# The order of steps in differential attention's slots: scaling first, turns ahead of logits in every fourth slot, memory evictions one slot sooner, the last key turn later

## The chip, the cores and the metric

The kernel runs on one core of a Trainium2 chip. The metric is device time in microseconds (us) of one execution; lower is better. TensorE (PE in the profile) multiplies and turns (transposes) tiles, ScalarE (ACT) computes exponentials and copies, VectorE (DVE) does two-operand arithmetic and reductions, GpSimd (POOL) small extra work, and SyncE (SP) issues most of the transfers. Each engine runs its own list of instructions in order, and semaphores tie the lists together.

## What is computed

Two transformer blocks in a row on 512 tokens of width 1024, in float32. The first has two layers; the change lies in its second layer, which has differential attention (6 heads, two logit maps each) beside attention to a memory of 256 rows (4 heads). Cut to what matters:

```python
def diff_attention(q1, q2, k1, k2, v, lam):          # per block of 128 queries
        s1 = jnp.einsum('bqhd,bkhd->bhqk', a1, k1).astype(jnp.float32) * scale
        s2 = jnp.einsum('bqhd,bkhd->bhqk', a2, k2).astype(jnp.float32) * scale
        p1 = jax.nn.softmax(jnp.where(mask, s1, -jnp.inf), axis=-1)
        p2 = jax.nn.softmax(jnp.where(mask, s2, -jnp.inf), axis=-1)
        p = (p1 - lam * p2).astype(v.dtype)
        return jnp.einsum('bhqk,bkhe->bqhe', p, v)

def memory_attention(q, mem_n, w_mem_kv, q_gain, k_gain):
    sc = jnp.einsum('bshd,bmhd->bhsm', qh, k).astype(jnp.float32) * (MEM_HEAD_DIM ** -0.5)
    p = jax.nn.softmax(sc, axis=-1).astype(v.dtype)
    o = jnp.einsum('bhsm,bmhd->bshd', p, v)
```

## The kernel before

Large products are float32 in effect: each operand is split into a high and a low part, and a product is three matmuls (`mm3`, lines 1092 to 1094). ScalarE makes the high parts of the weights (line 1759), VectorE the low parts (lines 2252 and 2254).

The second layer's attention runs as a list of slots, `PLAN_B`. In each slot TensorE first does one piece of a projection (query, key, value, or output product; `PIECES`, at most four in a row share a weight slab), and then the steps that the list gives for that slot. ScalarE and VectorE walk the same list, each doing its own share of the same steps in the same order. They also take a share of the weights' splitting in every second slot.

The steps of the list:

- Memory attention, units 0 to 7: `s` logits, `x` exponential, `y` scaling, `t` turn of the weights (TensorE line 1216, ScalarE line 1820, VectorE line 2317), `v` product with the values, `e` eviction of it (ScalarE line 1832, VectorE line 2324). A pair of units shares one `v` and one `e`.
- `rt` turns rotated rows of queries or keys, one 128-row tile at a time, on TensorE (line 1436), and ScalarE takes the result (line 2000).
- Differential attention, units 0 to 23; unit u is query tile u % 4 of head u // 4, and works on 128, 256, 384 or 512 keys. `D`: two logit products on TensorE (lines 1455 and 1458), then the maxima on VectorE (lines 2637 and 2641). `X`: the two exponentials on ScalarE (line 2026), then on VectorE the reciprocals of the sums (lines 2646 and 2649). `M`: ScalarE scales the second map (line 2015), then VectorE combines both (line 2654). `T`: TensorE turns the combined weights (line 1464), ScalarE makes the high part (line 2008), VectorE the low part (line 2659). `V`: product with the values, after which `O` (ScalarE lines 2032 and 2035) takes it out.
- Once a head: `sums` (TensorE line 1418), `R` (a reciprocal root over ScalarE lines 1771 and 1773 and VectorE), `N` (TensorE line 1486, VectorE line 2673), `C` (ScalarE line 2043), and the residual's `add` (VectorE line 2684).

`unit_at(s)` gives unit s its slot. Units 0 to 7 come three slots apart. Units 8 to 23 are dense: four units in six slots. In each such group of four, the logits stand in the first, second, fourth and fifth slot, and the exponential in the slot after its logits, ahead of the next unit's logits where both meet. `D` of a unit waits for `X` of the unit before, since both use the same two PSUM banks (`q.wait_ge(S("df_exp"), 2 * u)`, line 1445). `T`, `t`, `rt` and `N` share one PSUM bank in the list's order: each of them waits until the one before it has been read out. ScalarE's `O` waits for TensorE's `V`, and VectorE's `M` for ScalarE's `M`.

Of the kernel before, what the change touches and what calls it, by code (L numbers as in the profile page):

```python
# [15 lines left out]
T = 512  # L16
D = 1024
# [80 lines left out]
def build(nc, cols, ins, out):  # L98
# [10 lines left out]
    def place(shape, dt, offset):  # L109
        names[0] += 1  # L110
        return nc.alloc_sbuf_tensor_at(f"sb{names[0]}", shape, dt, offset=offset)
# [303 lines left out]
    PLAN_B = [[] for _ in range(len(PIECES) + 8)]  # L415
    KEY_ROWS = 69

    def unit_at(s):
        return 44 + 3 * s if s < 8 else 74 + (s - 8) * 3 // 2 if s < 24 else 97 + (s - 24) * 3 // 2
# [8 lines left out]
    for t in range(4):  # L428
        PLAN_B[16 + t].append(("qt", t))
        PLAN_B[24 + 3 * t].append(("rt", "QB", t))  # L430
        PLAN_B[(38, 39, 41, 42)[t]].append(("rt", "KB", t))
        PLAN_B[52 + t].append(("rt", "QA", t))
        PLAN_B[71 + t + (t > 0)].append(("rt", "KA", t))
        PLAN_B[77 + t].append(("ev", "va", t))
    for u in range(8):
        s = 20 + 3 * u
        PLAN_B[s].append(("s", u))
        PLAN_B[s + 1].append(("x", u))
        PLAN_B[s + 2].append(("y", u))
        PLAN_B[s + 5].append(("t", u))  # L440
        if u % 2 == 1:
            PLAN_B[s + 7].append(("v", u // 2))
            PLAN_B[s + 8].append(("e", u // 2))
    for s in range(30):
        p = unit_at(s)
        if s >= 4 and s % 4 == 0 and s <= 24:
            PLAN_B[p].append(("V", s // 4 - 1, 0))
        if s >= 8 and s % 4 == 0:
            PLAN_B[p].append(("sums", s // 4 - 2))
        if s < 24:  # L450
            PLAN_B[p].append(("D", s))
        if 0 <= s - 2 < 24:
            PLAN_B[p].append(("T", s - 2))
        if 0 <= s - 1 < 24:
            PLAN_B[p].append(("M", s - 1))
        if s < 24:
            PLAN_B[p + 1].append(("X", s))
        if s >= 6 and s % 4 == 2:
            PLAN_B[p + 1].append(("V", s // 4 - 1, 1))
        if s >= 6 and s % 4 == 2:  # L460
            PLAN_B[p + 1].append(("O", s // 4 - 1))
        if s >= 8 and s % 4 == 0:
            PLAN_B[p + 1].append(("R", s // 4 - 2))
        if s >= 9 and s % 4 == 1:
            PLAN_B[p + 1].append(("N", s // 4 - 2))
            PLAN_B[p + 2].append(("C", s // 4 - 2))
# [354 lines left out]
    KA = place([128, 4, 512], F32, s1_off)  # L821
# [2171 lines left out]
```

## Time and profile before

| | us |
|---|---|
| median of 3 runs | 1722.68 (1721.58 to 1723.02) |
| the profiled execution | 1722.6 |
| its span, first to last instruction | 1720.8 |
| TensorE busy | 1680.7 |
| VectorE busy | 1222.5 |
| ScalarE busy | 842.6 |
| the stretch of the second layer's attention | about 540 to 780 us in the span |

The profile is of one execution. Busy time of an engine is the time in which it has an instruction under way; TensorE's clock is given beside it as a share of full speed (mean 0.994). In the rows, a start is counted from the span's start; a number in brackets behind a row is how long the engine had been idle, with what ended the wait.

### The profile page before, as it was taken

What the parts mean: (1) busy time and instruction counts of PE and PEld (TensorE: products, weight loads), DVE (VectorE), ACT (ScalarE), POOL (GpSimd) and SP (SyncE); (2) the same over time, 40 slices, a digit from 0 to 9 for tenths busy, and PEclk for the clock granted to TensorE, in tenths of its full rate; (3) what the DMA queues carried; (4) which work ended last, traced back from release to release, by engine and by line L of the source; (5) the groups of instructions that cost most, each with busy time, mean ns of one, the idle gap of its engine ahead of it and who ended that gap; (6) DMA issues with size and microseconds to landing.
All of it is one profiled execution on the core that took longest, in us unless ns stands there. A gap on an engine that the chain in (4) does not pass through costs nothing.

```text
span 1720.8 us, 20867 instructions
## 1 busy us (share of the span) xinstructions
PE 1680.7 (98%) x7882; PEld 1373.8 (80%) x7882; DVE 1222.5 (71%) x1868; ACT 842.6 (49%) x1405; POOL 62.8 (4%) x116
## 2 busy tenths in 40 slices
PE   7999999999999999899999999999999999999998
PEld 6778888888888777668888888888877788888886
DVE  6667458687888666765777778988885645766666
ACT  7444344343445776764444444555876523333342
POOL 0000000000001121000000000013100000000000
PEclk9999999999999999999999999999989999999999
DMA  9322443333412212116142424058500262234212
GB/s 329 86 74 93 140 123 95 111 92 107 132 52 51 77 51 73 40 47 187 47 146 62 149 69 124 13 128 192 115 26 25 87 209 73 63 122 123 71 46 79
DMA packets 200500, 169.02 MB, mean 98 GB/s; under 512 B 5776, under 2 KB 161808, under 8 KB 200144
## 3 DMA queue, kind: packets, MB, share of 16 engines
q1 hardware_dynamic: 194816, 157.31, 29.8%
q0 software_dynamic: 4576, 8.85, 2.9%
q10 hardware_dynamic: 1008, 1.53, 0.3%
q8 instruction: 63, 1.03, 0.2%
q14 instruction: 37, 0.30, 0.1%
HBM read 157.96 MB, written 2.10 MB: 93 GB/s over the span
## 4 chain that ended last, share of the span: by engine, by line
PE 90%; DVE 5%; ACT 3%; issue 1%; DMA 0%; POOL 0%; DVEq 0%; SPq 0%; ACTq 0%
PE ps L1092 28%; PE ps L1094 28%; PE ps L1093 28%; PE ps L1156 1%; PE ps L1455 1%; PE ps L1575 1%; DVE sb L2254 1%; ACT sb L1759 1%; PE ps L1587 1%; ACT sb L2026 1%; DVE sb L2733 1%; PE ps L1109 0%; DVE sb L2782 0%; PE ps L1110 0%; PE ps L1113 0%
## 5 line engine op out<-in xcount | busy, mean ns | idle before, releaser
L1092 PE MATMUL ps<-sb,sb 128*128 128x512 f32 (+2 forms) x2292 | 887.9, 390 | 11.6 <-DVE sb L2254 10.1
L1094 PE MATMUL ps<-sb,sb 128*128 128x512 f32 (+2 forms) x2292 | 874.5, 383 | 0.0
L1093 PE MATMUL ps<-sb,sb 128*128 128x512 f32 (+2 forms) x2292 | 873.9, 383 | 0.0
L2254 DVE TENSOR_TENSOR sb<-sb,sb 128x1024 fp32r<-128x1024 f32 (+1 forms) x414 | 405.1, 998 | 223.5 <-ACT sb L1759 223.0
L1759 ACT ACTIVATE sb<-sb 128x1024 fp32r<-128x1024 f32 (+1 forms) x414 | 349.1, 870 | 386.1 <-PE ps L1094 380.1
L1092 PEld LDWEIGHTS ps<-sb,sb 128*128 128x128 f32 (+1 forms) x2292 | 429.4, 189 | 105.2 <-DVE sb L2254 10.8
L1094 PEld LDWEIGHTS ps<-sb,sb 128*128 128x128 f32 (+1 forms) x2292 | 429.0, 188 | 84.8
L1093 PEld LDWEIGHTS ps<-sb,sb 128*128 128x128 f32 (+1 forms) x2292 | 429.5, 189 | 80.7
L2485 DVE TENSOR_TENSOR sb<-sb,sb 128x1024 fp32r<-128x1024 f32 x70 | 85.5, 1222 | 47.5 <-ACT sb L1933 45.2
L1928 ACT ACTIVATE sb<-sb 128x512 f32<-128x512 f32 x64 | 40.3, 631 | 131.3 <-DVE sb L2537 131.3
L2467 DVE TENSOR_TENSOR sb<-sb,sb 128x1024 f32<-128x1024 f32 x80 | 95.2, 1218 | 0.6
L2502 DVE TENSOR_TENSOR sb<-ps,sb 128x512 f32<-128x512 f32 x120 | 76.1, 682 | 0.3 <-PE ps L1094 0.3
L2733 DVE SCALAR_TENSOR_TENSOR sb<-sb,sb,sb 128x512 f32<-128x512 f32 x90 | 67.4, 749 | 2.0
L1933 ACT ACTIVATE sb<-sb 128x1024 fp32r<-128x1024 f32 x56 | 58.7, 1048 | 9.0 <-DVE sb L2479 8.9
L2537 DVE SCALAR_TENSOR_TENSOR sb<-ps,sb 128x512 f32<-128x512 f32 x64 | 43.6, 685 | 9.0 <-PE ps L1094 9.0
L2479 DVE TENSOR_TENSOR sb<-sb 128x1024 f32<-128x1024 f32 x40 | 48.7, 1218 | 0.1
L2210 ACT ACTIVATE sb<-sb 128x512 f32<-128x512 f32 x22 | 13.9, 632 | 70.6 <-DVE sb L2912 70.5
L1069 POOL DMA_DIRECT2D sb<-sb x29 | 25.1, 879 | 430.9 <-ACT sb L2101 390.1
L2252 DVE SCALAR_TENSOR_TENSOR sb<-sb,sb,sb 128x512 fp32r<-128x512 f32 x40 | 29.6, 751 | 11.8 <-ACT sb L1759 11.6
L1765 ACT ACTIVATE sb<-sb 128x1024 f32<-128x1024 f32 x26 | 27.5, 1059 | 8.5 <-DVE sb L2684 4.9
L2026 ACT ACTIVATE sb<-ps,sb,sb 128x128 f32<-128x128 f32 (+3 forms) x48 | 29.1, 613 | 5.1 <-DVE sb L2641 5.1
L2912 DVE TENSOR_TENSOR sb<-ps,sb 128x512 f32<-128x512 f32 x22 | 15.1, 687 | 20.8 <-PE ps L1094 20.8
(215 smaller groups left out, 1167.7 us busy)
## 6 DMA issues: line engine op xcount, KB each, us to landing
sb<-in_w_up SPq DMA_DIRECT2D x86, 512.0 KB, 4.0
sb<-in_w_down SPq DMA_DIRECT2D x86, 512.0 KB, 4.8
sb<-in_w_gate SPq DMA_DIRECT2D x22, 512.0 KB, 3.9
sb<-in_a_w_in SPq DMA_DIRECT2D x20, 512.0 KB, 3.8
sb<-in_w_in SPq DMA_DIRECT2D x20, 512.0 KB, 3.8
sb<-in_w_o SPq DMA_DIRECT2D x16, 512.0 KB, 3.7
sb<-sb POOLq DMA_DIRECT2D x29, 256.0 KB, 4.6
sb<-in_w_mem_kv SPq DMA_DIRECT2D x8, 512.0 KB, 8.7
```

The source lines that it names most:

```text
L1092: mm(ps, lh, rh, start=start, stop=False, **k)
L1093: mm(ps, lh, rl, start=False, stop=False, **k)
L1094: return mm(ps, ll, rh, start=False, stop=stop, **k)
L1759: act(WH[i % N_SPLIT][:, a], raw[:, a], ACT.Copy, scale=g).then_inc(S("w_hi"), parts)
L1933: act(AR[(7 * g + j) % 4][0], a_of(l, g, j)[0], ACT.Copy).then_inc(S("h_hi"), 1)
L2026: act(E, banks[B.lb + w][:, 0:nk], ACT.Exp, bias=M[:, 2 + w:3 + w], scale=r[:, w:w + 1], accum_out=M[:, 4 + w:5 + w]).then_inc(S("df_exp"), 1)
L2254: tt(lo, raw, hi, ALU.subtract).then_inc(S("w_lo"), parts)
L2467: tt(db[d][a][:, :], db[b][a][:, :], db[c][a][:, :], ALU.subtract).then_inc(S("t_sum"), 1)
L2479: tt(d, x, y, op).then_inc(S("hs"), 1)
L2485: tt(lo, a_of(l, g, j)[0], hi.bitcast(F32), ALU.subtract).then_inc(S("h_lo"), 1)
L2502: tt(x, y, x, ALU.add).then_inc(S("res"), 1)
L2733: stt(CV[:, j, :], GL[:, j, k:k + T], col("convw", 4 * k + j), CV[:, j, :], ALU.mult, ALU.add).then_inc(S("tap"), 1)
```

## The change

The change alters only the list `PLAN_B`; every instruction stays, with the same operands.

```diff
-        PLAN_B[71 + t + (t > 0)].append(("rt", "KA", t))
+        if t < 3:
+            PLAN_B[71 + t + (t > 0)].append(("rt", "KA", t))
...
         if u % 2 == 1:
-            PLAN_B[s + 7].append(("v", u // 2))
-            PLAN_B[s + 8].append(("e", u // 2))
+            PLAN_B[s + 7] += [("v", u // 2), ("e", u // 2)]
     for s in range(30):
         p = unit_at(s)
+        if 0 <= s - 1 < 24:
+            PLAN_B[p].append(("M", s - 1))
         if s >= 4 and s % 4 == 0 and s <= 24:
             PLAN_B[p].append(("V", s // 4 - 1, 0))
         if s >= 8 and s % 4 == 0:
             PLAN_B[p].append(("sums", s // 4 - 2))
-        if s < 24:
-            PLAN_B[p].append(("D", s))
-        if 0 <= s - 2 < 24:
-            PLAN_B[p].append(("T", s - 2))
-        if 0 <= s - 1 < 24:
-            PLAN_B[p].append(("M", s - 1))
+        unit = [("D", s)] if s < 24 else []
+        turned_ = [("T", s - 2)] if 0 <= s - 2 < 24 else []
+        PLAN_B[p] += turned_ + unit if s % 4 == 1 else unit + turned_
         if s < 24:
             PLAN_B[p + 1].append(("X", s))
+        if s == 8:
+            PLAN_B[p + 1].append(("rt", "KA", 3))
```

So `M` of the unit before goes from the end of a slot's unit steps to their start; `T` goes ahead of `D` for units 1, 5, 9 and so on; the memory evictions `e` go one slot sooner, into the slot of their product `v`; and the last turn of keys goes behind `X` of unit 8 within its slot. The changed file has one line more, so its line numbers are one higher from there on.

TensorE, around the logits of unit 17, before (line 1455 and 1458 are `D`, 1464 is `T`; the 1092 row starts the next piece):

```order
3147 L1093 MATMUL ps<-sb_62,sb_167 128x512
3148 L1094 MATMUL ps<-sb_59,sb_168 128x512
3149 L1455 MATMUL ps<-sb_153,sb_151 128x256 x2
3150 L1458 MATMUL ps<-sb_70,sb_69 128x128 x2
3151 L1464 MATMUL ps<-sb_64,sb_127 128x128 x4
3152 L1092 MATMUL ps<-sb_60,sb_125 128x512
```

And in the changed kernel:

```order
3147 L1094 MATMUL ps<-sb_62,sb_167 128x512
3148 L1095 MATMUL ps<-sb_59,sb_168 128x512
3149 L1465 MATMUL ps<-sb_64,sb_127 128x128 x4
3150 L1456 MATMUL ps<-sb_153,sb_151 128x256 x2
3151 L1459 MATMUL ps<-sb_70,sb_69 128x128 x2
3152 L1093 MATMUL ps<-sb_60,sb_125 128x512
```

The turn of unit 15 now stands ahead of the logits of unit 17.

VectorE, from the reciprocals of unit 17 to those of unit 19, before (2637 and 2641 are the maxima of `D`, 2659 is `T`, 2654 is `M`, 2673 is `N`):

```order
756 L2649 TENSOR_SCALAR sb_147<-sb_147,sb_144 128x1
757 L2673 SCALAR_TENSOR_TENSOR sb_135<-ps,sb_144,sb_133 128x512
760 L2637 TENSOR_REDUCE sb_147<-ps 128x1 x2
762 L2659 TENSOR_TENSOR sb_130<-ps,sb_129 128x128
763 L2654 SCALAR_TENSOR_TENSOR sb_127<-sb_127,sb_147,sb_128 128x256
...
765 L2649 TENSOR_SCALAR sb_147<-sb_147,sb_144 128x1
766 L2637 TENSOR_REDUCE sb_147<-ps 128x1 x2
767 L2641 SCALAR_TENSOR_TENSOR sb_147<-sb_147,sb_146 128x2
768 L2659 TENSOR_TENSOR sb_130<-ps,sb_129 128x2x128
769 L2654 SCALAR_TENSOR_TENSOR sb_127<-sb_127,sb_147,sb_128 128x384
```

And in the changed kernel:

```order
756 L2650 TENSOR_SCALAR sb_147<-sb_147,sb_144 128x1
757 L2674 SCALAR_TENSOR_TENSOR sb_135<-ps,sb_144,sb_133 128x512
760 L2655 SCALAR_TENSOR_TENSOR sb_127<-sb_127,sb_147,sb_128 128x256
761 L2638 TENSOR_REDUCE sb_147<-ps 128x1 x2
763 L2660 TENSOR_TENSOR sb_130<-ps,sb_129 128x128
...
765 L2650 TENSOR_SCALAR sb_147<-sb_147,sb_144 128x1
766 L2655 SCALAR_TENSOR_TENSOR sb_127<-sb_127,sb_147,sb_128 128x384
767 L2638 TENSOR_REDUCE sb_147<-ps 128x1 x2
768 L2642 SCALAR_TENSOR_TENSOR sb_147<-sb_147,sb_146 128x2
769 L2660 TENSOR_TENSOR sb_130<-ps,sb_129 128x2x128
```

The combination of units 17 and 18 now stands ahead of the maxima of units 18 and 19.

ScalarE, around the second memory eviction, before (1842 is `x`, 1832 is `e`, 1820 is `t`, 1827 is `y`):

```order
376 L1773 ACTIVATE sb_77<-sb_77 128x4
377 L1842 ACTIVATE sb_148,sb_147<-ps,sb_147,sb_145 128x256 x2
378 L1759 ACTIVATE sb_58<-sb_57,sb_65 128x512
379 L1832 ACTIVATE sb_125<-ps 64x256 x2
380 L1820 ACTIVATE sb_149<-ps 128x4x128
381 L1827 ACTIVATE sb_148<-sb_148,sb_147 128x256 x2
```

And in the changed kernel:

```order
376 L1774 ACTIVATE sb_77<-sb_77 128x4
377 L1833 ACTIVATE sb_125<-ps 64x256 x2
378 L1843 ACTIVATE sb_148,sb_147<-ps,sb_147,sb_145 128x256 x2
379 L1760 ACTIVATE sb_58<-sb_57,sb_65 128x512
380 L1821 ACTIVATE sb_149<-ps 128x4x128
381 L1828 ACTIVATE sb_148<-sb_148,sb_147 128x256 x2
```

The eviction now stands ahead of the exponential of memory unit 5; the same holds for the other three.

## Rows read from the trace of the kernel before

**Rows 1.** The page, section 1: busy time, share of the span, instructions.

```profile
PE 1680.7 (98%) x7882; PEld 1373.8 (80%) x7882; DVE 1222.5 (71%) x1868; ACT 842.6 (49%) x1405; POOL 62.8 (4%) x116
```

**Rows 2.** Waits of TensorE, 540 to 790 us: total, times, longest (us).

```profile
PE ps L1455 <- ACT sb L2026: 3.7, 4, 1.7
PE ps L1486 <- DVE sb L2659: 2.4, 4, 0.8
PE ps L1436 <- DVE sb L2317: 1.9, 1, 1.9
```

**Rows 3.** Stretches, TensorE: length, busy (count), granted clock, DMA share, GB/s.

```profile
613.00:617.00 4.00, 4.00 (x14) 0.57 0.22 72
690.00:692.00 2.00, 0.38 (x4) 1.00 0.00 0
```

**Rows 4.** Timeline of the group of units 16 to 19: start, length, instruction.

```profile
724.24 0.95 PE L1418 MATMUL ps<-sb,sb 128*128 128x2 f32 x8
...
728.22 0.70 PE L1455 MATMUL ps<-sb,sb 64*128 64x256 f32 x4 [0.68 <-ACT sb L2026]
...
730.09 0.39 ACT L2015 ACTIVATE sb<-sb,sb 128x128 f32<-128x128 f32 x1
...
730.11 0.76 DVE L2637 TENSOR_REDUCE sb<-ps 128x1 f32<-128x256 f32 x2
...
730.97 0.69 DVE L2659 TENSOR_TENSOR sb<-ps,sb 128x512 fp32r<-128x512 f32 x1
...
731.72 0.65 PE L1486 MATMUL ps<-sb,sb 128*128 128x128 f32 x4 [0.75 <-DVE sb L2659]
...
733.60 0.63 ACT L2043 ACTIVATE sb<-sb 128x512 fp32r<-128x512 f32 x1 [0.78 <-DVE sb L2673]
...
734.71 1.02 DVE L2637 TENSOR_REDUCE sb<-ps 128x1 f32<-128x384 f32 x2
...
737.69 1.13 PE L1455 MATMUL ps<-sb,sb 64*128 64x512 f32 x4
...
738.42 0.63 ACT L2035 ACTIVATE sb<-sb 128x512 f32<-128x512 f32 x1
...
738.91 1.29 DVE L2637 TENSOR_REDUCE sb<-ps 128x1 f32<-128x512 f32 x2 [1.09 <-PE ps L1458]
...
739.56 0.61 ACT L2015 ACTIVATE sb<-sb,sb 128x384 f32<-128x384 f32 x1
...
740.59 0.77 ACT L2026 ACTIVATE sb<-ps,sb,sb 128x512 f32<-128x512 f32 x1
...
742.60 0.95 PE L1418 MATMUL ps<-sb,sb 128*128 128x2 f32 x8
```

**Rows 5.** Timeline: the sums that open units 12 to 15, and those behind unit 23.

```profile
705.62 1.05 PE L1418 MATMUL ps<-sb,sb 128*128 128x2 f32 x8
...
760.80 1.05 PE L1418 MATMUL ps<-sb,sb 128*128 128x2 f32 x8 [0.49 <-ACT sb L2026]
...
764.31 0.63 PE L1464 MATMUL ps<-sb,sb 128*128 128x128 f32 x4 [0.68 <-DVE sb L2654]
```

**Rows 6.** Timeline around the first two memory products.

```profile
593.52 0.56 ACT L1842 ACTIVATE sb<-ps,sb,sb 128x256 f32<-128x256 f32 x1
...
594.25 0.28 PE L1094 MATMUL ps<-sb,sb 128*128 128x256 f32 x1
...
600.64 0.46 ACT L2000 ACTIVATE sb<-ps,sb 128x256 f32<-128x256 f32 x1
...
612.06 0.44 PE L1436 MATMUL ps<-sb,sb 128*128 128x128 f32 x2 [1.93 <-DVE sb L2317]
```

**Rows 7.** Timeline around units 1 to 3 and the query turns.

```profile
634.77 0.55 ACT L2026 ACTIVATE sb<-ps,sb,sb 128x256 f32<-128x256 f32 x1
...
642.92 0.66 PE L1436 MATMUL ps<-sb,sb 128*128 128x128 f32 x4 [0.23 <-DVE sb L2659]
...
648.77 0.66 PE L1436 MATMUL ps<-sb,sb 128*128 128x128 f32 x4 [0.16 <-DVE sb L2659]
```

## What was predicted

> **What bounds the kernel now.** The page comes first: TensorE is busy for 98% of the span, VectorE 71% [rows 1]. So an edit is worth what it does to TensorE's idle time and clock. The change adds and removes no instruction, so only waits can move. The waits of TensorE over the second layer's attention come next. Three kinds matter [rows 2]: logits `D` that wait for the exponential of the unit before (3.7 us, 4 times), the turn `N` that waits for VectorE's half of `T` (2.4 us, 4 times), and one query or key turn `rt` that waits 1.9 us for VectorE's half of a memory turn `t`. Then the clock by stretches: behind the 1.9 us wait it is 0.57 over 4 us, which costs 4 x 0.43 = 1.7 us on top, while a wait of 1.66 us inside 690 to 692 left it at 1.00 [rows 3]. The timeline of one dense group, last, shows what stands around each wait [rows 4]. Some 12 us in all could be had.
>
> **The dense groups (units 8 to 23).** I take the group of units 16 to 19. It runs from its `sums` at 724.24 to the next at 742.60, 18.36 us [rows 4]. I walk the new order through it with the old durations, putting the start of `sums` at 0 and handing over between engines in 0.05 us (the `N` at 731.72 starts 0.06 after the end of the VectorE row at 730.97 [rows 4]). Next starts on one engine overlap the last by about 0.1 us.
>
> What it gains. `T` of unit 15 goes ahead of `D` of unit 17 and fills the wait of 0.68 us. `M` of unit 15 no longer holds up ScalarE ahead of `X` of unit 16. The next piece starts some 0.7 us sooner, and `N` follows about 0.6 us sooner, since the turn it waits for is earlier.
>
> What it costs. `D` on VectorE feeds the exponential and so the next `D` on TensorE; in the new order it stands behind `M`, and `M` on VectorE stands behind `M` on ScalarE.
>
> - Unit 17's maxima. Before, they start at 730.11, that is 5.87. Now ahead of them come, from the end of unit 16's reciprocals (about 5.2; VectorE has the split of a weight half and `R` there as before): ScalarE's `M` 0.39, its half of `T` (about 0.6), and VectorE's half of `T`, 0.69, which waits for it [rows 4]. 5.2 + 0.3 + 0.6 + 0.7 gives 6.8: 0.9 us later, and `X` of unit 17 with them.
> - Unit 18's maxima. Before 734.71, 10.47. `X` of unit 17 is late by 0.9, so its reciprocals, `N`'s VectorE part and ScalarE's `C` (0.63, before at 733.60 [rows 4]) are late: `C` starts about 10.2. `M` of unit 17 waits in line behind `C` on ScalarE, and VectorE's maxima wait for it. 10.2 + 0.5 (`C` less the overlap) + 0.5 + 0.5 (an estimate, between the 0.39 and 0.61 of units 16 and 18) gives 11.65: 1.2 us later. `X` of unit 18 then ends at 14.3, and `D` of unit 19 on TensorE starts at 14.35, against 13.45 before (737.69 [rows 4]). Here the gain of 0.7 is gone and 0.9 lost.
> - Unit 19's maxima. In this slot ScalarE also has `O`, two copies of 0.6 each (the second at 738.42 [rows 4]), and it stands ahead of `M`. Before, VectorE took unit 19's maxima at 738.91, straight from TensorE, while ScalarE was still at `O` and got to `M` at 739.56. Now: `X` of unit 18 ends 14.3, `O` to 15.45, `M` on ScalarE 0.61, `M` on VectorE as long, maxima at 16.55. Before it was 14.67. `X` of unit 19 starts 1.5 later (1.29 of maxima, the small product, a handover), at 18.07 against 16.35 before (740.59 [rows 4]), and lasts 1.6; the next `sums` waits for its end and starts at 19.73 against 18.36.
>
> So the group takes 1.4 us more. As a check from below: even if `X` of unit 18 came in time and TensorE kept its 0.7, `O` would end at 738.5 and `M` on both engines put unit 19's maxima at 739.65 instead of 738.91, 0.7 later; less 0.4 us that lie between the end of `X` and `sums` (740.59 + 1.6 = 742.2 against 742.60 [rows 4]) that still is about +0.25 us a group. A gain of a whole group isn't in reach.
>
> For the other groups: units 12 to 15 take 18.62 now (705.62 to 724.24) and get the same 19.73, +1.1; units 20 to 23 take 18.20 (742.60 to 760.80), +1.5 [rows 4, 5]. In units 8 to 11 ScalarE's evictions of values and the last key turn set the pace; the key turn behind `X` of unit 8 turns the 1.7 us wait [rows 2] into one of about 0.75, which brings TensorE forward by 1.1 us, and unit 11's late `M` takes it back: +0.1. Behind unit 23, `T` waits 0.68 us for `M` [rows 5], which is now ahead of the other steps: -0.7. Sum of the dense part: 0.1 + 1.1 + 1.4 + 1.5 - 0.7 = +3.4 us.
>
> **The memory evictions.** `e` on ScalarE now waits for the product `v` of its own slot, with `x` behind it. At the first, ScalarE was free at 593.52 and took `x`; `v` ends at 594.53 [rows 6]. ScalarE stalls 1.0 us in a stretch in which it is busy without a gap, so the taking out of a query turn at 600.64 [rows 6] comes 1.0 later, and TensorE's next user of that bank, the turn of memory unit 3 just behind it, waits 0.9. At the second, `e` fits into an idle time and leaves the slot where the 1.93 us wait ends at 612.06 [rows 6]: there ScalarE saves 0.7 and VectorE 0.9. With the 0.9 from before, TensorE gets through at about 611.8: -0.3, and the wait shrinks to 0.8. As 1.66 us left the clock at full speed [rows 3], I take the 1.7 us of half clock as gone: -1.7. At the fourth, `e` waits 1.3 us for `v` and takes 0.7, and `X` of unit 1, at 634.77 before [rows 7], starts 2.0 later. VectorE and ScalarE are full for the next 6 us there. The maxima of unit 2 come 1.5 us later (0.4 of it for `M` of unit 1 ahead), unit 0's turn behind them, and the query turn at 642.92, which already waits for that turn, with it: +1.45. `M` of unit 2 ahead of unit 3's maxima adds another 0.65 at the turn at 648.77 [rows 7]. Together -0.3 - 1.7 + 2.1 = +0.1.
>
> Bounds. Where a stall of ScalarE is absorbed, the query turns cost nothing, not +2.1; where nothing is, the first eviction's 0.9 adds to it. The half clock returns 0 or 1.7, or a new stretch costs another 1.7. The dense part lies between four times the 0.25 from below, less 0.7, and four times 1.5: +0.3 to +6.
>
> **The clock.** The row at 690 to 692 says that a wait of 1.66 us can pass at full clock, and the new waits in a dense group are at most 1.1 [rows 3]. The Trainium skill ("TensorE: Matmul & The Clock Gate", Part 1: The HAM clock gate) says that the throttled state is the default and activity releases it; by that alone each group with more idle time than before could lose its clock once. With one half-clock stretch a group of 1.7 us the sum would be 3.5 + 4 x 1.7, some 1733; by the row it is nothing. I go by the row.
>
> **The sum.** +3.4 + 0.1 = +3.5 us on the profiled 1722.6, 1726.1; on the median of 1722.68, which is 0.1 above it, 1726.2. A difference of 0.2%, 3.4 us, is about what a measurement of this kernel tells from no change, and the forecast lies on that edge.
>
> **The rivals.**
>
> - Half the delay is absorbed (chance 0.27). VectorE is at 71%, and other steps may close up behind `M` sooner than I walk. Then the dense groups cost about 0.7 each and the query turns 1: 4 x 0.7 - 0.7 + 1 - 2 = +1.1, 1723.8. For it: no step is longer, only the order. Against: each link of the walk is a wait that the list makes.
> - A clock loss (0.17). The half-clock stretch stays where it is, or comes back beside the query turn at 642.9, whose wait grows to about 1.7 us, the length of the wait that just passed. 1726.2 + 1.7 = 1727.9. It decides as soon as a wait is as long as the 1.93 of now.
> - The turns ahead fill their waits and nothing is lost (0.08). It needs `M` to be ready before the maxima in each slot, that is ScalarE at least 1.2 us sooner in the slot with `O`. Then the four waits of `D` (3.7), half of those of `N` (1.2), the 0.7 behind unit 23, and the 2.0 at the memory turn are all gained: -7.6, 1715.
> - The forecast itself, delays of 1 to 1.5 us in three groups with the half clock gone: 0.48.
>
> **How the numbers follow.** The forecast and the clock rival span 1724.5 to 1729.3; the absorbed case reaches down to 1722.3. 1722.3 to 1729.3 leaves out the gain of the third rival and the tails of the others, about 2 in 10. Faster by over 0.2% only by the third rival and none of the others: 0.08. Slower: the clock rival nearly whole, 0.15, and a little over half of the forecast, 0.28: 0.43. Within 0.2%: the rest, 0.49.
>
> **What would show it right or wrong.** Right: from one `sums` to the next 19.7 us instead of 18.4 and 18.2 in the groups of units 16 and 20; the maxima of the 512-key units released by ScalarE's `M` and no longer by TensorE; `D` of the 512-key unit waiting about 1 us for ScalarE; clock at 1.00 from 613 to 617. Wrong: periods at or under 18.4 (the absorbed case or the gain), a key or query turn without waits at 642.9 and 648.8, or a clock under 1.00 anywhere between 640 and 760.

## The result and the profile after

| kernel | median (us) | runs | profiled span (us) |
|---|---|---|---|
| before | 1722.85 (1721.58 to 1724.78) | 4 | 1720.8 |
| after | 1731.47 (1730.44 to 1732.40) | 4 | 1728.9 |

The change makes the kernel slower: ratio 1.0055, 95% interval 1.0043 to 1.0067. The prediction said 1726.2, with 1729.3 as the upper end of its range. It gave slower by more than 0.2% a chance of 0.43, faster 0.08, and no clear change 0.49. So the direction that it leaned to was right, though it was not its likeliest outcome. The size was off by 5.3 us, and the range missed.

The page of the kernel after has nearly the same busy times as [rows 1], spread over 8.1 us more. In this kernel all line numbers are one higher than before.

```profile
PE 1681.5 (97%) x7882; PEld 1373.7 (79%) x7882; DVE 1224.6 (71%) x1868; ACT 842.9 (49%) x1405; POOL 63.2 (4%) x116
```

The waits of TensorE from 540 to 790 us, against [rows 2]: total, times, longest.

```profile
PE ps L1456 <- ACT sb L2027: 4.4, 4, 2.0
PE ps L1437 <- DVE sb L2660: 2.5, 2, 1.7
PE ps L1487 <- DVE sb L2660: 2.3, 3, 0.8
PE ps L1093 <- POOL sb L1064: 2.0, 2, 1.0
PE ps L1419 <- ACT sb L2027: 1.2, 4, 0.4
PE ps L1437 <- DVE sb L2318: 1.1, 1, 1.1
PE ps L1093 <- DVE sb L2660: 1.1, 1, 1.1
```

`D` waits longer (L1456), `sums` waits at the end of every group (L1419), the query turns wait (L1437 on L2660), and a kind that was not there before appears: a piece of a weight product (L1093) waits for GpSimd (L1064, the low part of a head's output). It is 2.0 us, and the prediction has no word about it.

The stretches of TensorE, against [rows 3]: length, busy time, granted clock, DMA share, GB/s.

```profile
613.00:617.00 4.00, 4.00 (x22) 1.00 0.38 121
762.00:766.00 4.00, 2.96 (x15) 1.00 0.00 0
766.00:768.00 2.00, 1.12 (x8) 1.00 0.00 0
768.00:772.00 4.00, 4.00 (x17) 0.57 0.02 4
```

The half clock at 613 to 617 is gone, as predicted. But one of the same length and depth, 0.57 over 4 us, now stands at 768 to 772, so that nothing is gained by it.

The timeline of the group of units 16 to 19, against [rows 4]: start, length, instruction.

```profile
731.96 0.40 ACT L2016 ACTIVATE sb<-sb,sb 128x128 f32<-128x128 f32 x1 [0.75 <-DVE sb L2650]
...
736.87 0.63 ACT L2044 ACTIVATE sb<-sb 128x512 fp32r<-128x512 f32 x1 [0.69 <-DVE sb L2674]
...
737.35 0.68 DVE L2255 TENSOR_TENSOR sb<-sb,sb 128x512 fp32r<-128x512 f32 x1
737.41 0.49 ACT L2016 ACTIVATE sb<-sb,sb 128x256 f32<-128x256 f32 x1
737.58 1.60 POOL L1064 TENSOR_TENSOR sb<-sb,sb 128x512 fp32r<-128x512 f32 x1 [19.12 <-ACT sb L2044]
...
737.95 1.51 DVE L2655 SCALAR_TENSOR_TENSOR sb<-sb,sb,sb 128x256 f32<-128x256 f32 x1
739.38 1.01 DVE L2638 TENSOR_REDUCE sb<-ps 128x1 f32<-128x384 f32 x2
...
742.09 1.13 PE L1456 MATMUL ps<-sb,sb 64*128 64x512 f32 x4 [2.04 <-ACT sb L2027]
...
743.73 0.62 DVE L2655 SCALAR_TENSOR_TENSOR sb<-sb,sb,sb 128x384 f32<-128x384 f32 x1 [1.24 <-ACT sb L2016]
...
744.26 1.28 DVE L2638 TENSOR_REDUCE sb<-ps 128x1 f32<-128x512 f32 x2
```

The row to see is the one at 737.95. VectorE's half of `M` of unit 17 lasts 1.51 us, for 256 columns, while the 384 columns of unit 18 at 743.73 take 0.62. Its share on ScalarE was done at 737.90, so it began with its inputs ready, while GpSimd's subtraction of 737.58 was running, and it ended at 739.46, 0.28 us behind that one's end at 739.18. The maxima of unit 18 stand behind it, then `X`, then `D` of unit 19 at 742.09, which has waited 2.04 us. In the kernel before, VectorE had the maxima beside the same subtraction, with one input, from PSUM, and `M` only after its end (two more rows of before):

```profile
734.30 1.61 POOL L1063 TENSOR_TENSOR sb<-sb,sb 128x512 fp32r<-128x512 f32 x1 [17.33 <-ACT sb L2043]
...
736.05 0.47 DVE L2654 SCALAR_TENSOR_TENSOR sb<-sb,sb,sb 128x256 f32<-128x256 f32 x1
```

The four such `M` of the dense part take 1.14, 1.19, 1.51 and 1.19 us after, and 0.47 or 0.48 before.

In the other groups, and where `sums` opens units 20 to 23 and closes unit 23:

```profile
718.51 0.50 PE L1093 MATMUL ps<-sb,sb 128*128 128x512 f32 x1 [0.98 <-POOL sb L1064]
...
726.74 1.05 PE L1419 MATMUL ps<-sb,sb 128*128 128x2 f32 x8 [0.29 <-ACT sb L2027]
...
766.52 0.38 PE L1093 MATMUL ps<-sb,sb 128*128 128x256 f32 x1 [1.11 <-DVE sb L2660]
...
767.85 1.36 PE L1419 MATMUL ps<-sb,sb 128*128 128x2 f32 x8 [0.35 <-ACT sb L2027]
```

The time from one `sums` to the next leaves out what came before the dense part. Single profiles of kernels whose program is the same up to 685 us reach that point up to 1.2 us apart (685.07 in one of the runs below, 686.22 before), while their groups agree to 0.02 us. The table has these times for before, after and all runs, each from one profiled execution (the tail is from the `sums` behind unit 23 to the last one).

| kernel | 8–11 | 12–15 | 16–19 | 20–23 | tail | sum |
|---|---|---|---|---|---|---|
| before | 19.40 | 18.62 | 18.36 | 18.20 | 13.03 | 87.61 |
| after | 20.06 | 20.43 | 20.72 | 20.39 | 13.76 | 95.36 |
| e1 scaling last | 19.34 | 19.22 | 18.59 | 18.79 | 13.00 | 88.94 |
| e2 scaling first alone | 20.55 | 19.62 | 19.90 | 19.59 | 12.14 | 91.80 |
| e3 evictions alone | 19.41 | 18.64 | 18.35 | 18.20 | 13.03 | 87.63 |
| e4 after, GpSimd one fill | 19.38 | 19.71 | 19.69 | 19.67 | 12.15 | 90.60 |
| e5 after, GpSimd two fills | 19.39 | 19.98 | 19.69 | 19.95 | 12.14 | 91.15 |
| e6 turns ahead alone | 19.64 | 19.21 | 18.58 | 18.77 | 12.98 | 89.18 |
| e7 scaling first at a group's start | 18.01 | 18.27 | 17.75 | 17.58 | 12.13 | 83.74 |
| e8 after, not beside GpSimd | 18.98 | 20.15 | 19.32 | 20.12 | 13.52 | 92.09 |
| e9 key turn alone | 18.56 | 18.63 | 18.35 | 18.20 | 13.01 | 86.75 |
| e10 first beside the output copies | 19.88 | 19.37 | 19.19 | 19.37 | 13.73 | 91.54 |
| e11 e7, second eviction alone | 18.03 | 18.28 | 17.74 | 17.60 | 12.13 | 83.78 |
| e12 first beside GpSimd | 20.18 | 19.17 | 19.50 | 18.73 | 13.01 | 90.59 |

Of the 8.1 us, 7.75 lie here.

The table does not hold all of a kernel's time, and the medians show it: e1, e2 and e6 are 2.8, 7.6 and 3.1 us above before by their medians, but 1.3, 4.2 and 1.6 by the table. Part of the difference is TensorE's clock far behind this layer. Between 1250 and 1320 us it was at half in every profile for some microseconds. Its lost share times the length comes to 5.1 or 5.2 us in most, 6.8 in e1, e5, e6 and e11, and 10.3 in e10. Executions of one kernel differ in this way too: the five of e4 took 1725.6 to 1729.1 us, the slower two at a mean clock of 0.993 and the others at 0.994 or 0.995. Whether the change moves these later stretches, no run here separates. So the steps are read from the groups, and the medians only say faster or slower.

### The profile page after: what moved, and what is told of

Same layout as the page of the kernel before. It is cut to its first block, busy times and chain, and to the rows that moved or that the text cites. A ratio compares the mean times of both kernels' runs of the same rounds, so it can differ in the third digit from the quotient of the medians.

```text
span 1728.9 us, 20867 instructions
## 1 busy us (share of the span) xinstructions
PE 1681.5 (97%) x7882; PEld 1373.7 (79%) x7882; DVE 1224.6 (71%) x1868; ACT 842.9 (49%) x1405; POOL 63.2 (4%) x116
## 4 chain that ended last, share of the span: by engine, by line
PE 88%; DVE 6%; ACT 5%; issue 1%; DMA 0%; POOL 0%; DVEq 0%; SPq 0%; ACTq 0%
PE ps L1093 28%; PE ps L1095 27%; PE ps L1094 27%; ACT sb L2027 1%; DVE sb L2638 1%; PE ps L1576 1%; PE ps L1157 1%; PE ps L1588 1%; DVE sb L2255 1%; ACT sb L1760 0%; PE ps L1110 0%; PE ps L1111 0%; PE ps L1114 0%; DMA sb<-in_w_mem_kv 0%; DVE sb L2783 0%
## 5 line engine op out<-in xcount | busy, mean ns | idle before, releaser
L1093 PE MATMUL ps<-sb,sb 128*128 128x512 f32 (+2 forms) x2292 | 887.6, 390 | 14.6 <-DVE sb L2255 10.3
L1093 PEld LDWEIGHTS ps<-sb,sb 128*128 128x128 f32 (+1 forms) x2292 | 428.9, 188 | 109.5 <-DVE sb L2255 10.9
```

Source lines behind the costliest of these rows:

```text
L1093: mm(ps, lh, rh, start=start, stop=False, **k)
```

## The experiments

Theory: `M` first costs by the order, as walked, and by one thing that the walk did not have, VectorE and GpSimd reading SBUF at once (the clash, from here on). The rivals were that `T` ahead or the evictions carry the loss, or that GpSimd is only a bystander. Each ratio is to the kernel before, timed on the same chip in the same rounds; its median was 1722.03 beside e1 to e4, 1721.78 beside e5 to e8, and 1722.35 beside e9 to e12. Line numbers shift by up to five between runs, as the edits add or take lines.

### The parts: e1, e2, e3

e1 is the changed kernel with `M` back behind `D` and `T`:

```diff
-        if 0 <= s - 1 < 24:
-            PLAN_B[p].append(("M", s - 1))
         if s >= 4 and s % 4 == 0 and s <= 24:
...
         PLAN_B[p] += turned_ + unit if s % 4 == 1 else unit + turned_
+        if 0 <= s - 1 < 24:
+            PLAN_B[p].append(("M", s - 1))
```

> The changed kernel with one part undone: M goes back behind D and T in its slot; T ahead of D in every fourth slot, the earlier evictions and the later key turn stay. Theory A (M ahead of the maxima is the whole loss): the three dense groups of units 12 to 23 fall from 20.4 to 20.7 us each back to 18.4 or less, VectorE's scaling of the 256-key unit is back at 0.48 us, and the kernel ends 2 to 4 us below the kernel before (1719 to 1721), since the 1.7 us of half clock and the 0.7 us wait before the turn stay gained. Rival B (the turn ahead of the logits is what hurts, because VectorE's half of the turn now stands ahead of the maxima): periods stay above 19 us and the kernel at or above 1726.

Measured: 1724.86, ratio 1.0016 (1.0008 to 1.0025). It lies between the two, so neither expectation holds: most of the loss leaves with `M` first, but what stays is still a loss and not a gain. Its rows, on TensorE:

```profile
690.34 0.66 PE L1465 MATMUL ps<-sb,sb 128*128 128x128 f32 x4 [1.33 <-ACT sb L2001]
...
716.58 0.50 PE L1093 MATMUL ps<-sb,sb 128*128 128x512 f32 x1 [0.98 <-POOL sb L1064]
...
727.80 0.63 PE L1465 MATMUL ps<-sb,sb 128*128 128x128 f32 x4 [0.68 <-DVE sb L2655]
```

`T` of unit 15, moved ahead of `D` of unit 17 (the row at 727.80), waits for `M` for the same 0.68 us that `D` waited for `X` in [rows 4], and the piece that needs GpSimd's low part comes too soon. In units 8 to 11, `T` now stands right behind the last key turn and waits 1.33 us for ScalarE to take that turn's result (the row at 690.34).

e2 is the kernel before with `M` first and nothing else:

```diff
     for s in range(30):
         p = unit_at(s)
+        if 0 <= s - 1 < 24:
+            PLAN_B[p].append(("M", s - 1))
...
             PLAN_B[p].append(("T", s - 2))
-        if 0 <= s - 1 < 24:
-            PLAN_B[p].append(("M", s - 1))
```

> The kernel before with only M moved to the start of each slot's steps. Theory A: it alone brings most of the loss, periods of 19.5 us or more for units 12 to 23, VectorE's scaling of the 256-key unit 1.1 to 1.5 us long beside GpSimd's subtraction, and 4 to 8 us over the kernel before (1727 to 1731), with the half-clock stretch still near 613 us. Rival B: within 2 us of the kernel before.

Measured: 1729.60, ratio 1.0044 (1.0031 to 1.0058), and +4.2 us in the table's sum. The profiled execution, at 1726.63, was the fastest of its four. Theory A, with the half-clock stretch near 613 us still there (0.74 from 612 to 616). `M` first carries most of the loss by itself, and the scaling of the 256-key units is as long as in the changed kernel (1.12, 1.21, 1.51 and 1.21 us).

e3 is the kernel before with the evictions sooner and nothing else:

```diff
-            PLAN_B[s + 7].append(("v", u // 2))
-            PLAN_B[s + 8].append(("e", u // 2))
+            PLAN_B[s + 7] += [("v", u // 2), ("e", u // 2)]
```

> The kernel before with only the memory evictions one slot sooner. By the prediction's steps: the turn at 612 waits about 1.1 us instead of 1.9, the half clock behind it (1.7 us) is gone, a wait of about 0.7 us comes in at 601, and the query turn at 642.9 waits about 1.1 us longer without M's share: -1 us in all (1721.5 to 1722.5), or 1.7 higher if the half clock only moves. Rival (evictions sooner cost more than they bring): over 1724.5.

Measured: 1722.11, ratio 1.0004 (0.9995 to 1.0013), no difference. The half clock is gone, and most of its time went where the prediction put it, into a later query turn and into the wait at 601. First a stretch behind the turn, then the query turn in the timeline:

```profile
612.00:616.00 4.00, 4.00 (x25) 1.00 0.16 37
```

```profile
641.91 0.66 PE L1435 MATMUL ps<-sb,sb 128*128 128x128 f32 x4 [1.31 <-DVE sb L2658]
```

### The clash with GpSimd: e4, e5, e8, e12

e4 is the changed kernel in which GpSimd, instead of subtracting, fills the low part with zeros; the output lacks that part.

```diff
-                    TTT(lo[:, :], OT[:, :], hi[:, :].bitcast(F32), ALU.subtract).then_inc(S("sub_lo"), 1)
+                    e.memset(lo[:, :].bitcast(F32), 0.0).then_inc(S("sub_lo"), 1)
```

> The changed kernel with GpSimd's subtraction for the low part of each head's result (128x512, two inputs from SBUF) replaced by a fill with zeros, so the low part is left out of the output product. Theory C (VectorE's scaling stands still while GpSimd reads SBUF): VectorE's scaling of the 256-key unit falls from 1.14 to 1.51 us to 0.48, the periods of units 12 to 23 from 20.4 to 20.7 us to the 19.7 of the prediction's walk, and the kernel loses 2 to 3.5 us (1728 to 1729.5). Rival D (the scaling is long for another reason, such as its place behind the weight's split): it stays over 1.1 us and the kernel within 0.7 us of 1731.

Measured: 1726.44, ratio 1.0031 (1.0019 to 1.0043), and a span 5.2 us under that of after. Theory C in its rows, with more time lost than its 2 to 3.5 us, since the half clock of the tail went too. The scaling is back at 0.48, although it still starts while GpSimd is at work:

```profile
735.50 0.53 POOL L1064 MEMSET sb<- 128x512 f32 x1 [19.15 <-ACT sb L2044]
...
735.90 0.48 DVE L2655 SCALAR_TENSOR_TENSOR sb<-sb,sb,sb 128x256 f32<-128x256 f32 x1
```

One fill is shorter than the subtraction too, so that the low part also comes sooner. e5 makes it late again with a second fill behind the first, still without reading anything (and still without the low part in the output):

```diff
-                    TTT(lo[:, :], OT[:, :], hi[:, :].bitcast(F32), ALU.subtract).then_inc(S("sub_lo"), 1)
+                    e.memset(lo[:, :].bitcast(F32), 0.0).then_inc(S("fill"), 1)
+                    q.wait_ge(S("fill"), g + 1)
+                    e.memset(lo[:, :].bitcast(F32), 0.0).then_inc(S("sub_lo"), 1)
```

> The changed kernel with GpSimd's subtraction (the low part of a head's output, 1.3 to 1.6 us, two SBUF inputs) replaced by two fills of 0.53 us each, the second waiting for the first: GpSimd is busy about as long and its low part is as late as in the changed kernel, but it reads nothing. The output lacks that low part. In the run with one fill, VectorE's scaling of a 256-key unit took 0.48 us instead of 1.14 to 1.51, but the low part was also sooner, so two causes went at once. Theory A (both read SBUF and stand in each other's way): the scaling takes 0.48 us here too, D of the 512-key units waits 2.8 us in all and not 4.4; the pieces behind T still wait about 0.8 us twice for the low part; 1727 to 1728. Rival B (it is the late low part that costs, and the long scaling hides behind it): as the changed kernel, 1730 or more. Rival C (GpSimd's being at work stops VectorE, whatever it reads): the scaling stays above 1 us.

Measured: 1728.47, ratio 1.0044 (1.0028 to 1.0059), 0.5 us above theory A's range. Theory A's three rows came: the scaling takes 0.48, pieces wait 0.80 us twice for the low part, and `D` waits less (1.8 us in all, where 2.8 was expected). In the rows the scaling runs beside both fills:

```profile
736.40 0.53 POOL L1064 MEMSET sb<- 128x512 f32 x1 [18.85 <-ACT sb L2046]
736.80 0.48 DVE L2657 SCALAR_TENSOR_TENSOR sb<-sb,sb,sb 128x256 f32<-128x256 f32 x1
736.99 0.52 POOL L1066 MEMSET sb<- 128x512 f32 x1
```

So the two causes come apart. From e4 to e5 the table's sum grows by 0.55 us: that is the late low part. From e5 to after it grows by 4.2: 1.7 of it is the half clock of the tail, and the other 2.5 is left for the clash. Up to 0.4 of that can still be the low part, since two fills end a little sooner than the subtraction and the two waits for it are 0.80 and not 0.98 us. Rival C is out by the rows. Rival B is out by them too: `D` waits 1.8 us and not 4.4, and each group is 0.4 to 1.0 us shorter than in after. The medians alone would not settle B, as the intervals of the two ratios overlap. The Trainium skill ("SBUF — State Buffer", Who interferes with whom) has the rule: "A DVE instruction with two SBUF inputs contends with a GpSimd instruction that reads SBUF", and one that only writes does not. The trace agrees on all its sides: 1.14 to 1.51 us beside the subtraction, 0.48 beside fills, and 1.02 us, as everywhere, for maxima from PSUM beside it [rows 4].

e8 is the changed kernel with `M` behind again in the one slot of four in which GpSimd subtracts:

```diff
-        if 0 <= s - 1 < 24:
+        if 0 <= s - 1 < 24 and s % 4 != 2:
             PLAN_B[p].append(("M", s - 1))
...
         PLAN_B[p] += turned_ + unit if s % 4 == 1 else unit + turned_
+        if 0 <= s - 1 < 24 and s % 4 == 2:
+            PLAN_B[p].append(("M", s - 1))
```

> The changed kernel with M behind D and T again in one slot of four, that in which GpSimd subtracts (M of the 256-key unit). Theory A (that slot carries most of the loss): the scaling takes 0.48 us, D of the 512-key unit comes 2 us sooner and waits under 0.3, groups of 18.7 to 19.3 us instead of 20.4 to 20.7, 1725 to 1727. Rival B (the slot with O carries it): groups stay at 20 or more, 1729 to 1731.

Measured: 1729.08, ratio 1.0044 (1.0030 to 1.0058). Theory A is right in two groups (18.98 and 19.32 us) and wrong in the other two (20.15 and 20.12). There the piece behind `T` waits 0.98 us for the low part, as in after, and what the scaling gives back goes into that wait. The expectation had no term for it; the total came out outside its range.

e12 goes the other way, the kernel before with `M` first in that slot alone:

```diff
+        if 0 <= s - 1 < 24 and (s % 4 == 2):
+            PLAN_B[p].append(("M", s - 1))
...
-        if 0 <= s - 1 < 24:
+        if 0 <= s - 1 < 24 and not (s % 4 == 2):
             PLAN_B[p].append(("M", s - 1))
```

> The kernel before with M first in one slot of four, that in which GpSimd subtracts (M of the 256-key unit ahead of the maxima of the 384-key unit). Theory A (this slot costs by the order and by the clash with GpSimd): the scaling takes 1.1 to 1.5 us instead of 0.48, the maxima behind it come some 1.5 us later, D of the 512-key unit waits about 1 us, groups 0.7 to 1.2 us longer, 1725 to 1727. Rival B (TensorE's pieces cover it when T and the other M stand where they stood): groups within 0.3, under 1723.5.

Measured: 1725.81, ratio 1.0018 (1.0009 to 1.0027), groups longer by 0.78, 0.55, 1.14 and 0.53 us. Theory A, though two groups stay under its 0.7; `D` waits 6.4 us in all, against 3.7 before.

```profile
736.04 1.60 POOL L1065 TENSOR_TENSOR sb<-sb,sb 128x512 fp32r<-128x512 f32 x1 [17.88 <-ACT sb L2045]
736.41 1.51 DVE L2656 SCALAR_TENSOR_TENSOR sb<-sb,sb,sb 128x256 f32<-128x256 f32 x1
737.85 1.01 DVE L2639 TENSOR_REDUCE sb<-ps 128x1 f32<-128x384 f32 x2
740.55 1.13 PE L1457 MATMUL ps<-sb,sb 64*128 64x512 f32 x4 [1.06 <-ACT sb L2028]
```

### The other slots and steps: e6, e9, e10

e6 is the kernel before with `T` ahead of `D` in every fourth slot:

```diff
-        if s < 24:
-            PLAN_B[p].append(("D", s))
-        if 0 <= s - 2 < 24:
-            PLAN_B[p].append(("T", s - 2))
+        unit = [("D", s)] if s < 24 else []
+        turned_ = [("T", s - 2)] if 0 <= s - 2 < 24 else []
+        PLAN_B[p] += turned_ + unit if s % 4 == 1 else unit + turned_
```

> The kernel before with T ahead of D in every fourth slot alone. Theory A (T ahead gives no time back by itself: the wait of D moves behind it, and C is released by the exponential of unit 17 and no more by N, so that the low part is 1 us late for a piece in every second group): from one sums to the next about 0.6 us more in two or three of four groups, as in the run with scaling last, +1.3 in all; 1723.5 to 1724.5. Rival B (T fills the wait of D, and what the run with scaling last lost came from the key turn): groups of 17.7 to 18.0, 1720 to 1721.

Measured: 1724.92, ratio 1.0017 (1.0008 to 1.0026), groups longer by 0.24, 0.59, 0.22 and 0.57 us. Theory A, a little above its 1724.5. The two larger ones are those with the wait for the low part:

```profile
716.92 0.50 PE L1091 MATMUL ps<-sb,sb 128*128 128x512 f32 x1 [0.98 <-POOL sb L1062]
```

e10 is built as e12, with `s % 4 == 3`, the slot in which ScalarE copies the output twice.

> The kernel before with M first in one slot of four, that in which ScalarE copies the output twice (M of the 384-key unit ahead of the maxima of the 512-key unit). Theory A (what the prediction put as the least that this slot can cost: maxima 0.7 us later, 0.4 of it absorbed ahead of sums): groups 0.25 to 0.4 us longer, +1 to +1.6 in all, 1723.3 to 1724. Rival B (it is absorbed): groups as before within 0.1, 1722 to 1722.7. Rival C (the output slot carries the larger part of the loss): 0.8 us and more a group, above 1725.

Measured: 1726.89, ratio 1.0031 (1.0019 to 1.0043), groups longer by 0.48, 0.75, 0.83 and 1.17 us. It is nearer to rival C, against what I expected: above 1725, with 0.8 us a group as the mean of the four. (The profiled execution, at 1730.02, was the slowest of its six. Its tail holds a half-clock stretch too, 1.7 us.)

```profile
738.53 0.60 ACT L2034 ACTIVATE sb<-ps 128x512 f32<-128x512 f32 x1 [0.41 <-PE ps L1096]
739.16 0.63 ACT L2037 ACTIVATE sb<-sb 128x512 f32<-128x512 f32 x1
739.70 0.60 ACT L2017 ACTIVATE sb<-sb,sb 128x384 f32<-128x384 f32 x1
...
740.87 1.28 DVE L2639 TENSOR_REDUCE sb<-ps 128x1 f32<-128x512 f32 x2
```

The maxima start 16.00 us into the group (its `sums` is at 724.87) against 14.67 before, 1.33 later, and 0.83 arrives at the next `sums`. The 0.25 to 0.4 of the expectation was the prediction's check from below, which counted on TensorE keeping 0.7 us from `T` ahead; here there is none.

e9 is the kernel before with the last key turn behind `X` of unit 8:

```diff
-        PLAN_B[71 + t + (t > 0)].append(("rt", "KA", t))
+        if t < 3:
+            PLAN_B[71 + t + (t > 0)].append(("rt", "KA", t))
...
             PLAN_B[p + 1].append(("X", s))
+        if s == 8:
+            PLAN_B[p + 1].append(("rt", "KA", 3))
```

> The kernel before with the last key turn behind X of unit 8 alone. Theory A (the key turn held up ScalarE ahead of an exponential, as the prediction has it): the 1.66 us wait ahead of D of unit 9 shrinks to about 0.75 and the group of units 8 to 11 takes 18.3 us instead of 19.4, 1721 to 1722. Rival B (the wait only moves from D to the turn T behind it, as the 1.33 us in the run with scaling last suggests): the group takes 19.2 or more, no difference, 1722 to 1723. The run with scaling first at the group's start had 18.01 there, so by A nearly all of that gain is the key turn's, by B it is M's.

Measured: 1721.36, ratio 0.9992 (0.9983 to 1.0002); its group takes 18.56 us instead of 19.40. Theory A in kind, 0.84 us of the 1.1; `D` of unit 9 waits 0.23 us instead of 1.66, and `T` behind it 0.34. A gain of that size is under what the times resolve, but not under what the groups show.

### A faster version: e7, e11

e7 is the kernel before with the evictions (as e3), the key turn (as e9), and `M` first only in the slot that opens a group:

```diff
+        if 0 <= s - 1 < 24 and (s % 4 == 0):
+            PLAN_B[p].append(("M", s - 1))
...
-        if 0 <= s - 1 < 24:
+        if 0 <= s - 1 < 24 and not (s % 4 == 0):
             PLAN_B[p].append(("M", s - 1))
```

> The kernel before with the memory evictions one slot sooner and the last key turn later, and with M first only in the slots that open a group (M of units 11, 15, 19 and of the last unit), where no output copies stand on ScalarE and no subtraction on GpSimd; T stays behind D. Theory A (M first is paid for only beside O and beside GpSimd): D of the second unit of a group comes 0.3 us sooner, 4 times; T behind the last unit no longer waits 0.7; the evictions give 1.0; sum -2.9, 1719 to 1720. Rival B (M first costs in every slot, since the maxima stand behind it): groups 0.5 us longer each, 1723 or more.

Measured: 1717.89, ratio 0.9977 (0.9968 to 0.9986): faster, and by 1.1 us more than theory A's 1719. `D` of the second unit waits 0.3 us once, and otherwise not at all. In the third group it starts 3.36 us behind `sums`, against 3.98 before (728.22 less 724.24 [rows 4]), 0.6 sooner and not 0.3:

```profile
722.00 0.95 PE L1422 MATMUL ps<-sb,sb 128*128 128x2 f32 x8
...
725.36 0.70 PE L1459 MATMUL ps<-sb,sb 64*128 64x256 f32 x4
```

e11 is e7 with only the second of the four evictions sooner:

```diff
-            PLAN_B[s + 7] += [("v", u // 2), ("e", u // 2)]
+            PLAN_B[s + 7].append(("v", u // 2))
+            PLAN_B[s + 7 + (u != 3)].append(("e", u // 2))
```

> The kernel with M first at a group's start and the key turn later, and with the memory eviction sooner at one memory product of four, the second, where ScalarE was idle. Theory A (only that eviction gives something: its wait shrinks from 1.9 to about 1.1 or goes and the half clock behind it is gone, while the first eviction's wait of 0.70 at 601 and the added 1.1 at 642 were the price of the others): 1.5 to 2 us under the run with all four, 1716 to 1717. Rival B (the evictions depend on one another: without the first one's delay TensorE reaches the turn at 612 sooner and waits the 1.9 again, with the half clock): 1718 or more.

Measured: 1716.94, ratio 0.9969 (0.9958 to 0.9981), the fastest here. Against e7 it is 2.4 us less in the profiled span and 1 us in the medians, which were taken beside different runs of before, and the intervals of the two ratios overlap. Theory A's rows came; that e11 is faster than e7 is likely but not shown by the times. Its waits from 540 to 800 us have lost the 0.7 at 601 and the 1.3 at 642, and the half clock is gone as well:

```profile
PE ps L1441 <- DVE sb L2322: 1.2, 1, 1.2
...
PE ps L1441 <- DVE sb L2664: 0.4, 2, 0.2
```

## Why the prediction was wrong

**The step that failed** is in the walk, at unit 18's maxima: "10.2 + 0.5 (`C` less the overlap) + 0.5 + 0.5 (an estimate, between the 0.39 and 0.61 of units 16 and 18)". The last 0.5 is VectorE's `M` of unit 17, and it measured 1.51 (1.14 to 1.19 in the other groups). The change moves it to a place where GpSimd subtracts. I looked only at ScalarE's and VectorE's lines, and took its length from rows in which GpSimd was idle. GpSimd does not occur in the prediction at all.

With GpSimd's reads taken away (e4), the steps of the walk fall where it put them, counted from `sums` at 724.69: the maxima of unit 18 at 11.60 (11.65 in the walk), `D` of unit 19 at 14.32 (14.35), the maxima of unit 19 at 16.49 (16.55). In after they are at 12.64, 15.35 and 17.52.

The 3.4 us of the dense part became 7.75, and the runs split the difference:

| term | predicted | no reads by GpSimd (e4) | after |
|---|---|---|---|
| units 8 to 11 | +0.1 | -0.02 | +0.66 |
| units 12 to 15 | +1.1 | +1.09 | +1.81 |
| units 16 to 19 | +1.4 | +1.33 | +2.36 |
| units 20 to 23 | +1.5 | +1.47 | +2.19 |
| tail | -0.7 | -0.88 | +0.73 |
| sum | +3.4 | +2.99 | +7.75 |

With the reads of GpSimd gone, the sums hold to 0.12 us in every group and to 0.18 in the tail. (For units 8 to 11 that is luck, as told below.) The rest is another 0.55 (low part late) + 2.5 (clash, what is left of e5's difference) + 1.7 (half clock) = 4.75, and 2.99 + 4.75 = 7.74.

**The clock.** "by the row it is nothing. I go by the row" was wrong in the end. No stretch between 640 and 760 fell, as said, but behind waits of 1.11 and 0.35 us at 766 to 768 it did. The clock rival had the right price, 1.7, and the wrong place. The new stretch cannot be charged to the clash alone: in the profiled executions, e4 and e5 have the clash away and kept their clock there, but e8 lost it with `M` not beside GpSimd.

**The memory evictions** came as worked out in the rows of after: the wait at 612 is 1.13 (0.8 said), the new one at 601 is 0.70 (0.9), the turns at 642.3 and 648.8 wait 1.70 and 0.78 (1.68 and 0.81), and the clock from 613 to 617 is 1.00. The sum +0.1 fits e3, whose time shows no difference.

**The key turn** gave 0.84 of 1.1 by itself (e9). That unit 11's late `M` takes it back, as the prediction had it, is not what the runs show: in e1 `M` stands last and the group still takes 19.34 us, because `T` ahead waits there for the key turn (1.33 us). The +0.1 was close to e4's -0.02 by luck; the clash then made it +0.66.

**`T` ahead** was booked as a gain of 0.7 a group ahead of its costs. By itself it is a loss of 1.6 us in all (e6): its wait moves to `M`, and it sets the low part of GpSimd late. Only with `M` first does `T` not wait for it. The prediction has no term for the low part.

**The rivals.** The absorbed half and the gain are out. The range failed because its upper end held every step to the durations of before, and because it was narrower than the prediction's own bounds. Without the half clock the dense part grew by 6.05 us, right at the upper bound of +6, and another half-clock stretch of 1.7 stands among the bounds too, but the range ended at 1729.3.

Added up, e9, e6 and e2 give -0.86 + 1.57 + 4.19 = +4.9 in the table's sum. Of the remaining 2.85, 1.7 is the half clock; 1.15 is what the parts cost together beyond the sum of each alone. Of that, e1 shows 0.62 without `M` first, nearly all of it in units 8 to 11, where `T` ahead waits for the key turn; the other 0.5 was not taken further apart.

## What to carry to other kernels

When an instruction is moved, ask on every engine what will then run beside it, and not only what it waits for: its duration in the old place is a duration beside the old neighbours. In this kernel, VectorE's `M`, with two tensor inputs in SBUF, belongs beside a GpSimd that is idle or only writes (0.48 us), and the maxima, which read PSUM, can stand beside one that reads. A change that repeats in every slot is worth trying slot by slot: the same step was worth -3.0 us at a group's start (e7 against e9, by the table) and +3.0 beside GpSimd, and one eviction of four did at least as well as all four.

## What the runs showed of the hardware

VectorE's scaling, which has two tensor inputs in SBUF, ended 0.28 us behind the end of GpSimd's subtraction in all four groups of after (698.31, 718.74, 739.46 and 759.85 against 698.03, 718.46, 739.18 and 759.57). These four subtractions are not longer for it: three take 1.27 to 1.30 us and the third 1.60, as in before. That third one starts, in both kernels, while VectorE's own subtraction with two inputs is under way, 0.45 us ahead of that one's end (737.35 in the timeline above). In e4 a fill starts there 0.48 us ahead of the same end and takes the 0.53 us of every other fill. So in these rows it is the instruction that started second that became longer, and only where GpSimd reads. The profile gives GpSimd's spans only roughly, and this order was not tested by itself.

The half clock did not follow from the waits just ahead of it alone. The profiled executions of e5 and e8 have the same idle time on TensorE and the same two waits (1.36 and 0.35 us). e5 kept the clock, and e8 went to half of it. First the stretches of e5:

```profile
762.00:764.00 2.00, 0.64 (x4) 1.00 0.00 0
764.00:766.00 2.00, 1.65 (x13) 1.00 0.00 0
766.00:768.00 2.00, 2.00 (x14) 1.00 0.04 8
```

And those of e8:

```profile
762.00:764.00 2.00, 0.64 (x4) 1.00 0.00 0
764.00:766.00 2.00, 1.65 (x14) 1.00 0.00 0
766.00:768.00 2.00, 2.00 (x10) 0.68 0.00 0
768.00:770.00 2.00, 2.00 (x8) 0.50 0.04 8
```

That is one execution of each, and what sets them apart stays open. One wait that passed at full clock, as that of 1.66 us in [rows 3], is weak evidence that the next one will. A forecast has to carry such a 1.7 us as a chance wherever waits gather.
